# A dense SwiGLU layer whose first tile starts on parts of its input, and whose gate and up products take high and low rows in one moving operand

## The reference

```python
def swiglu(u, wg, wu, wd):
    return (jax.nn.silu(u @ wg) * (u @ wu)) @ wd
...
        x = x + gate * rmsnorm(y, g_norm[l, 1])
        shift, scale, gate = ada_modulation(c, w_ada[l, 1], b_ada[l, 1])
        h = rmsnorm(x, g_norm[l, 2]) * (1.0 + scale) + shift
        if l % 2 == 0:
            y = swiglu(h, w_gate_d[l // 2], w_up_d[l // 2], w_down_d[l // 2])
```

## Time and profile before

| what | value |
|---|---|
| median of three runs | 1752.06 us (1749.61 to 1752.65) |
| the profiled execution, its own time | 1752.9 us |
| its span, first to last instruction | 1751.1 us |
| TensorE busy | 1520.8 us, 87% of the span |
| VectorE, ScalarE, GpSimd busy | 712.4, 545.6, 63.1 us |
| mean granted clock of TensorE | 0.939 of 2.4 GHz |
| dense layer, first to last matmul start | 242.6 to 489.3 us |

### The profile page before, as it was taken

The page is one execution under the profiler, slowest core; times in us unless marked ns, Lnnn a source line. Parts: engine busy times, 40 slices in busy tenths (PEclk is TensorE's granted clock), DMA queues, the critical chain, the costliest instruction groups (busy, mean ns, idle before and its releaser), DMA issues.

```text
span 1751.1 us, 30564 instructions
## 1 busy us (share of the span) xinstructions
PE 1520.8 (87%) x12460; PEld 1226.9 (70%) x12461; DVE 712.4 (41%) x1020; ACT 545.6 (31%) x751; POOL 63.1 (4%) x66
## 2 busy tenths in 40 slices
PE   5999979999989998665658999979997569999794
PEld 3868769999976776554447875579995458888453
DVE  2263164555434532300017871166662036665112
ACT  2134043333222321100007750056551034554101
POOL 0010000000010001000000000000000000000002
PEclk9999989999999999887879999999998879999897
DMA  9625456545443436499999998997668995555694
GB/s 358 258 104 241 182 228 265 193 169 193 155 153 107 168 145 271 185 424 423 424 425 426 412 384 360 426 389 282 246 260 324 424 420 224 217 223 234 272 425 147
DMA packets 74565, 488.97 MB, mean 279 GB/s; under 512 B 9792, under 2 KB 13920, under 8 KB 16544
## 3 DMA queue, kind: packets, MB, share of 16 engines
q1 hardware_dynamic: 72176, 479.94, 68.1%
q10 hardware_dynamic: 1648, 4.59, 0.8%
q0 software_dynamic: 576, 2.10, 0.4%
HBM read 482.66 MB, written 3.93 MB: 278 GB/s over the span
## 4 chain that ended last, share of the span: by engine, by line
PE 78%; DMA 10%; issue 5%; DVE 3%; ACT 2%; POOL 1%; SPq 1%; ACTq 0%; POOLq 0%; DVEq 0%
PE PG L1315 9%; DMA ring<-in_experts 6%; PE Y L914 5%; PE PG L1359 5%; PE PG L1425 5%; PE TRB L1359 4%; PE Y L1327 4%; PE Y L1387 4%; PE Y L922 3%; PE Y L1176 3%; PE PG L878 3%; PE PG L879 3%; PE PG L880 3%; PE TRB L1365 3%; PE PG L1365 3%
## 5 line engine op out<-in xcount | busy, mean ns | idle before, releaser
L1315 PE MATMUL PG<-ring,mixT 128*32 128x128 f32 (+1 forms) x1920 | 120.7, 351 | 73.5 <-issue 73.5
L1315 PEld LDWEIGHTS PG<-ring,mixT 128*32 128x32 f32 (+1 forms) x1920 | 91.2, 138 | 105.7 <-issue 90.8
L1508 ACT ACTIVATE parts<-ring 128x2048 fp32r<-128x2048 f32 x84 | 158.4, 1906 | 11.8 <-PE Y L880 8.2
L2306 DVE COPY arena<-TRB 128x64 f32<-128x64 f32 (+1 forms) x70 | 17.6, 251 | 338.6 <-PE TRB L1301 338.6
L1508 ACT ACTIVATE rope<-PG 64x128 f32<-64x128 f32 (+2 forms) x84 | 27.1, 323 | 374.2 <-PE PG L1315 350.8
L1315 PE MATMUL PG<-arena,mixT 128*32 128x128 f32 (+1 forms) x1664 | 103.3, 358 | 38.7 <-issue 38.7
L878 PE MATMUL PG<-h_parts,parts 128*128 128x256 f32 x448 | 127.5, 285 | 10.2 <-DVE parts L2182 10.2
L879 PE MATMUL PG<-h_parts,parts 128*128 128x256 f32 x448 | 127.4, 284 | 0.0
L880 PE MATMUL PG<-h_parts,parts 128*128 128x256 f32 x448 | 127.2, 284 | 0.0
L1315 PEld LDWEIGHTS PG<-arena,mixT 128*32 128x32 f32 (+1 forms) x1664 | 80.4, 142 | 65.8 <-issue 51.9
L2182 DVE TENSOR_TENSOR parts<-ring,parts 128x2048 fp32r<-128x2048 f32 x42 | 95.9, 2292 | 25.5 <-ACT parts L1508 25.4
(11 more groups left out here) (361 smaller groups left out, 2750.3 us busy)
## 6 DMA issues: line engine op xcount, KB each, us to landing
ring<-in_experts SPq DMA_DIRECT2D x168, 1024.0 KB, 12.2
arena<-in_experts SPq DMA_DIRECT2D x168, 1024.0 KB, 15.8
ring<-in_weights SPq DMA_DIRECT2D x116, 1024.0 KB, 6.1
ring<-in_weights SPq DMA_DIRECT2D x4, 512.0 KB, 4.3
ypairs<-hT ACTq DMA_DIRECT2D x3, 512.0 KB, 6.3
tok<-in_x SPq DMA_DIRECT2D x1, 1024.0 KB, 9.1
result<-scr SPq DMA_DIRECT2D x2, 512.0 KB, 2.6
ring<-in_weights SPq DMA_DIRECT2D x2, 432.0 KB, 5.9
```

The lines of the kernel that those rows point to most:

```text
L1315: last = mm(bank[i * n:(i + 1) * n, 0:width], xe[:, k, 0:n], w[k // 4][:, k % 4, i * width:(i + 1) * width], start=(k == 0), stop=(k == KD ...
L1508: return nc.scalar.activation(out_, in_, func, **kw)
```

## The change

Four things are done.

- The post norms of both mixers and of the dense layer are fed sooner: ScalarE squares each block of Y when it is done (the last down tile signals `y_pair` three times), and for the mixers TensorE sums the first two blocks (four matmuls) ahead of the last projection block.
- ScalarE's and VectorE's splits of weight units 0 and 1 move ahead of the dense layer's pre norm; on ScalarE they stand between the squares of the post norm. ScalarE writes the high part of h straight from hT plus shift, in eight pieces, VectorE the low part in eight; the separate copies fall away.
- Tile 0 (`gu_first`) takes the high pieces of h for gate as each is ready, then up, then the low pieces. Its count of matmuls is unchanged.
- In tiles 1 to 27 the two products with the high weights (h high, h low) become one matmul of 512 columns, whose halves go to the two halves of a bank; gate has one bank, up the other. ScalarE then copies both low halves out (128 x 512), VectorE adds the high halves (128 x 512), and silu and the multiplication follow. TensorE waits for that sum (`gu_summed`) before the next gate and up tile; its wait for `act_ready` there falls away.

```diff
@@ -226,6 +226,7 @@
 
 OUT_ORDER = (2, 3, 0, 1)
 MIX_EARLY, MIX_LATE = (0, 1, 5, 6, 7), (2, 3, 4)
+POST_ORDER = [2 * c + j for c in OUT_ORDER for j in range(2)]
 
...
@@ -428,8 +429,8 @@
         qks = scr[:, 0:6, :]
         kro = scr[:, 6, :]
 
-        act = cut("dense", 2, T)
-        sg = cut("dense", 2, T)
+        gu_sum = cut("dense", 4, T).rearrange("p (a m) t -> p a m t", a=2)
+        low_part = cut("dense", 2, T)
         act_parts = parts[:, 0:4 * T].rearrange("p (a b t) -> p a b t", a=2, b=2)
         act_hi, act_lo = act_parts[:, 0, :, :], act_parts[:, 1, :, :]
         w_parts = [parts[:, 4 * T + i * KD * SW:4 * T + (i + 1) * KD * SW] for i in range(2 * SPLITS)]
...
@@ -814,18 +817,26 @@
                 for _ in range(n):
                     mm(bank[:, 0:T], ident, con[:, C_IOTA:C_IOTA + T], start=True, stop=True)
 
-            def stats(kind, n, q, between=None):
-
-
-                bank = take_tr((kind, n, "partial"))
-                if (kind, n) == ("pre", 3):
-                    busy(bank, 6)
-                for k in range(KD):
-                    if k % 2 == 0:
-                        pe.wait_ge(sq_ready, 4 * q + k // 2 + 1)
+            def partial(kind, n, q, at, to):
+
+                if at == 0:
+                    bank = take_tr((kind, n, "partial"))
+                    if (kind, n) == ("pre", 3):
+                        busy(bank, 6)
+                bank = tr[TR.bank((kind, n, "partial"))]
+                for i in range(at, to):
+                    k = POST_ORDER[i] if kind == "post" and n != 1 else i
+                    if i % 2 == 0:
+                        pe.wait_ge(sq_ready, 4 * q + i // 2 + 1)
                     g = 32 * (k % 4)
-                    last = mm(bank[g:g + 32, 0:T], ones[:, 0:32], scr[:, k, :], start=(k < 4), stop=(k >= 4))
-                last.then_inc(tr_full, 1)
+                    last = mm(bank[g:g + 32, 0:T], ones[:, 0:32], scr[:, k, :], start=(i < 4), stop=(i >= 4))
+                if to == KD:
+                    last.then_inc(tr_full, 1)
+
+            def stats(kind, n, q, between=None, at=0):
+
+
+                partial(kind, n, q, at, KD)
                 if between:
                     ada_rows(between)
                 bank = take_tr((kind, n, "total"))
...
+            def gu_first():
+
+                for d in range(2):
+                    pe.wait_ge(split_lo, d + 1)
+                    for k in range(KD):
+                        if d == 0:
+                            pe.wait_ge(h_ready, KD + k + 1)
+                        c = slice(k * SW, k * SW + P)
+                        mm(PG[:, d, 0:T], w_hi[d][:, c], h_hi[:, k, :], start=(k == 0), stop=False, skip_group_check=True)
+                        mm(PG[:, d, 0:T], w_lo[d][:, c], h_hi[:, k, :], start=False, stop=False, skip_group_check=True)
+                for k in range(KD):
+                    pe.wait_ge(h_lo_ready, k + 1)
+                    for d in range(2):
+                        last = mm(PG[:, d, T:2 * T], w_hi[d][:, k * SW:k * SW + P], h_lo[:, k, :],
+                                  start=False, stop=(k == KD - 1), skip_group_check=True)
+                return last
+
...
             def gu_tile(t):
 
-                bank = PG[:, t % 2, :]
+                if t == 0:
+                    return gu_first()
+                pe.wait_ge(gu_summed, t)
                 for m in range(2):
                     d = dense_use(KINDS[m], t // 2)
                     pe.wait_ge(split_lo, d + 1)
                     for k in range(KD):
-                        if t == 0 and m == 0 and k % (KD // 2) == 0:
-                            pe.wait_ge(h_lo_ready, k // (KD // 2) + 1)
-                        last = split_product(bank[:, m * T:(m + 1) * T], d % SPLITS, (h_hi[:, k, :], h_lo[:, k, :]),
-                                             k * SW + t % 2 * P, k == 0, k == KD - 1)
+                        c = slice(k * SW + t % 2 * P, k * SW + t % 2 * P + P)
+                        mm(PG[:, m, :].rearrange("p (i t) -> p i t", i=2), w_hi[d % SPLITS][:, c], h_parts[:, :, k, :],
+                           start=(k == 0), stop=False, skip_group_check=True)
+                        last = mm(PG[:, m, 0:T], w_lo[d % SPLITS][:, c], h_hi[:, k, :],
+                                  start=False, stop=(k == KD - 1), skip_group_check=True)
                 return last
 
...
@@ -900,6 +931,8 @@
                 for k in range(KD):
                     last = split_product(Yk[:, k, :], d % SPLITS, (act_hi[:, t % 2, :], act_lo[:, t % 2, :]),
                                          t % 2 * D + k * P, t == 0 and k % 2 == 0, t == FT - 1)
+                    if t == FT - 1 and k % 2 and k < KD - 1:
+                        last.then_inc(y_pair, 1)
                 return last
...
@@ -1197,6 +1230,8 @@
                 for b in range(2):
                     sc_over(2 + b)
                     pe.wait_ge(pj_free[b], len(PJ_LAYER) // 2 * (l + 1))
+                    if b:
+                        partial("post", 2 * l, 4 * l + 1, 0, KD // 2)
                     mixed(b, MIX_EARLY)
                     mixed(b, MIX_LATE).then_inc(y_full if b else out_read, 1)
...
@@ -1220,12 +1255,10 @@
 
 
             mixer(0)
-            stats("post", 0, 1)
+            stats("post", 0, 1, at=KD // 2)
             stats_pre(1, 2)
...
@@ -1525,9 +1558,14 @@
                     ae.wait_ge(hx_ready, KD * n + k + 1)
                     run(hT[:, k, :], hT[:, k, :], ACT.Identity, bias=mod[:, n, k:k + 1]).then_inc(h_ready, 1)
 
-            def squares_post(n, ready, value):
-                ae.wait_ge(ready, value)
-                for j in range(4):
+            def squares_post(n, *js):
+                for j in js:
+                    if n == 1:
+                        ae.wait_ge(*((y_pair, j + 1) if j < 3 else (down_done, FT)))
+                    elif j == OUT_ORDER[-1]:
+                        ae.wait_ge(y_full, 2 + n // 2)
+                    else:
+                        ae.wait_ge(out_read, (D // SW - 1) * (n // 2) + OUT_ORDER.index(j) + 1)
                     run(scr[:, 2 * j:2 * j + 2, :], Yk[:, 2 * j:2 * j + 2, :], ACT.Square).then_inc(sq_ready, 1)
 
...
             def split(d):
 
                 u = slot_of_dense(d)
@@ -1689,28 +1724,35 @@
                 run(w_hi[d % SPLITS], ring[:, slot_of[u], :, :].rearrange("p k c -> p (k c)"),
                     ACT.Copy).then_inc(split_hi, 1)
 
-            for i in range(2):
-                k = slice(i * KD // 2, (i + 1) * KD // 2)
-                ae.wait_ge(h_ready, KD + (i + 1) * KD // 2)
-                run(h_hi[:, k, :], hT[:, k, :], ACT.Copy).then_inc(h_hi_ready, 1)
-            for d in range(3):
-                split(d)
+            ae.wait_ge(*tr_done("mt4", 0))
+            squares_post(0, *OUT_ORDER[0:2])
+            split(0)
+            squares_post(0, OUT_ORDER[2])
+            split(1)
+            squares_post(0, OUT_ORDER[3])
+            squares_pre(1)
+            ada_rows(ADA_NORM[1])
+            for k in range(KD):
+                ae.wait_ge(hx_ready, KD + k + 1)
+                run(h_hi[:, k, :], hT[:, k, :], ACT.Identity, bias=mod[:, 1, k:k + 1]).then_inc(h_ready, 1)
+            split(2)
             for t in range(FT):
                 ae.wait_ge(gu_full, t + 1)
-                if t >= 2:
-                    ae.wait_ge(act_ready, t - 1)
-                run(sg[:, t % 2, :], PG[:, t % 2, 0:T], ACT.Silu).then_inc(silu_done, 1)
+                ae.wait_ge(gu_summed, t)
+                run(low_part, PG[:, :, T:2 * T], ACT.Copy).then_inc(low_out, 1)
+                ae.wait_ge(gu_summed, t + 1)
+                run(gu_sum[:, t % 2, 0, :], gu_sum[:, t % 2, 0, :], ACT.Silu).then_inc(silu_done, 1)
                 if t == 2:
                     ada_rows(ADA_DENSE)
                 for d in split_after(t):
                     split(d)
-            squares_post(1, down_done, FT)
...
@@ -2174,8 +2216,7 @@
                 mark(V.tensor_scalar(lam_v[:, l, 1:2], lam_v[:, l, 1:2], -LAM0[l], None, ALU.add))
             settle()
             mixer(0)
-            post(0)
-            pre(1)
+
             def split(d):
 
                 ve.wait_ge(split_hi, d + 1)
@@ -2183,21 +2224,27 @@
                                 ring[:, slot_of[slot_of_dense(d)], :, :].rearrange("p k c -> p (k c)"),
                                 w_hi[d % SPLITS].bitcast(F32), ALU.subtract).then_inc(split_lo, 1)
 
-            for i in range(2):
-                k = slice(i * KD // 2, (i + 1) * KD // 2)
-                ve.wait_ge(h_hi_ready, i + 1)
-                V.tensor_tensor(h_lo[:, k, :], hT[:, k, :], h_hi[:, k, :].bitcast(F32), ALU.subtract).then_inc(h_lo_ready, 1)
-            for d in range(3):
+            for d in range(2):
                 split(d)
+            post(0)
+            pre(1)
+            for k in range(KD):
+                ve.wait_ge(h_ready, KD + k + 1)
```

(12 more changed lines are left out.)

15 lines of the change are left out of this document (6 added, 9 removed).

## The result

| | before | changed |
|---|---|---|
| median, four runs each | 1752.11 us (1749.61 to 1752.65) | 1729.62 us (1726.26 to 1730.23) |
| profiled execution, its own time | 1752.9 | 1729.92 |
| its span | 1751.1 | 1728.1 |
| mean granted clock | 0.939 | 0.944 |

A forecast was written before the change was run, and what follows sets the result against it. It took the dense layer as bound by the number and spacing of its matmuls. Gains of 6.3 + 4.8 - 0.5 + 0.9 + 0.5 = 12.0 us gave 1740.9, as median 1740.0; range 1735 to 1747.

The forecast's parts named there:

- The start (6.3): Start of the dense layer: early weight splits let tile 1 start at 244.7 us, 6.3 us sooner, despite a later norm.
- The uncovered evacuation: Between dense tiles 0 and 1: tile 1 starts 1.7 us after tile 0's last matmul's start, with no down tile covering.
- Tiles 1 to 27 (4.8): Dense layer: each pair of 256-column matmuls becomes one of 512 columns at 0.2275 us, 4.8 us less in all.
- Tile 27 and the norms (-0.5, 0.9, 0.5): Tile 27's activations: 0.5 us more; post norm behind the dense layer 0.9 less, behind layer 1's mixer 0.5 less.
- (c): Dense tiles: the evacuation is not covered by the down tile, 27 us in all, 1767 us; chance 0.06.
- (a): Dense tiles 1 to 27: the wide matmul saves nothing, 7.2 us gained in all, 1744.9 us; chance 0.12.
- (b): Dense start: low clock for all of tile 0, and again after the 1.7 us pause; 8.0 gained, 1744.1 us; chance 0.10.
- (d): Layer 1 or the experts: the gain is given back waiting for weights at a fixed time, 1752 us; chance 0.06.
- Theory 2: From the experiments, not the prediction: experts start 11 us sooner and meet clock and DMA in another phase.

The follow-up runs named there:

- experiment 7: Changed kernel with ScalarE's copy of the low rows done twice per dense tile, then four times: 1740.50 us and 1743.23 us.
- place 68: Start of TensorE's experts loop in its listing, counted modulo 256: kernel before, 1752.11 us; changed kernel with 95 added waits, 1739.89 us.
- place 229: Same count, modulo 256: changed kernel, 1729.62 us, again 1730.32; kernel before with 161 instructions jumped over, 1741.92 us, or as executed waits, 1742.27.

## Why the prediction was right and wrong

**The start (6.3): right, 6.2.** The first matmul came at 234.2 us and tile 1 at 243.2; without the 1.6 us that the unchanged code ahead gained that is 235.8 and 244.8, against 235.3 and 244.7. The norm was 1.4 late, not 1.6 (218.68 plus the 1.6, against 218.86). Two errors cancel: the clock was also low from 220.8 to 224.2, inside the norm, which the sum put at nothing (the modulation product took 4.49 us instead of 3.66), and in tile 0 it was low for 3.4 us, not 4.5. The uncovered evacuation was right: tile 1 starts 1.69 us after tile 0's last matmul's start, 1.7 counted. Splits that fill a wait pay although they make the norm later, because h had to wait for the norm, and the first product for the splits.

**Tiles 1 to 27 (4.8): mis-sized, 2.5.** The step took 0.2275 us from 512-column products that follow each other. Here each alternates with a 256-column one, and the pair takes 0.3505 (5.608 / 16); less the 0.1188 of the narrow one (5.701 / 48) the wide one costs 0.2317. The prediction's own second reading, 0.231 from the line through 256 and 384 columns, was the right one, and it chose the other; the rest is the narrow product, taken at 0.1193 as the mean over both kinds of tile. The formula on the page "TensorE: Matmul & The Clock Gate" of the Trainium skill (section "Back-to-back issue gap"), which the page gives for a single matmul, would make it 2.5 ns a pair (the prediction has 2.6); measured are 2 x 118.8 - 231.7 = 5.9 ns, nearer to it than the 11.1 taken, and still more than double.

**Tile 27 and the norms (-0.5, 0.9, 0.5): about right.** 0.2 was lost at tile 27; with the norm behind the dense layer the stretch gained 3.4 less 2.5, that is 0.9 where 0.4 stood; layer 1's mixer 0.7, where 0.5 stood. That last one is luck in part: the early squares gained more than was counted, and the partial sums, counted as a gain, cost 0.8. The prediction set their price right, at 0.9, and overlooked that they buy nothing: once the squares are early, two sums are left behind the last square also when none is moved, as it had counted itself for the dense layer's norm.

**Rivals.** (c) didn't come: 1.35 us were spare. (a) holds by half. (b) didn't: after the pause of 1.41 us at tile 1 the clock stayed at 1.00, here and in all variants with that pause; in the two with pauses of 1.9 and 2.9 us (experiment 7) it fell. (d) was the only place in which the prediction looked at the later stages, and it asked only whether the gain could be lost to DMAs.

**The step that failed** is the one that isn't there: the sum sets the experts and the end at nothing, as work that "moves along". Some 10 of the 22.5 us come from there. Cause: 863 instructions fewer ahead of the loop over the experts move its code from place 68 to 229. Shown from both sides: the kernel before at place 229 takes 9 us less, the changed one at place 68 takes 10 more. At equal places the change is worth 1741.9 - 1730.3 = 11.6 us (place 229, one sitting) and some 10 to 12 at place 68 (1749.4 or 1752.1, less 1739.9): the 12.0 of the sum, partly by errors that cancel (1.6 of luck ahead, 2.3 too much for the wide products).

The Trainium skill's page "Runtime: NRT & Kernel Launch" (section "Instruction fetch mechanics") has instructions fetched in blocks of 16 KiB, 256 instructions, one after the other, and a taken branch whose target lies outside the blocks held stalls until that block has come. The trace agrees with the size (16,384 bytes, one to 254 executed in straight code), and the two runs with 256 instructions jumped over agree with a period of 256. A stall costs 4.4 us here ahead of expert 3, 6.4 ahead of expert 7, and 4.6 where the loop is left.

**Open** stays which branch misses which block at each place (the count has no real block edge in it), and what else moves a run: kernels of place 229 differ by up to 10 us from the last norm on (1042.6 to 1052.3, half of it ScalarE's stall above; 1042.6 to 1049.3 without that run), and unchanged code ahead of layer 0's projection ends 1.6 us apart. Theory 2, the phase, may be worth some of these 7 us; no run isolates it, and it doesn't explain the 9 and 10 us above. The edit moved the code of other engines too: at a branch in expert 6 VectorE pauses for 5.3 to 5.6 us in the three kernels made from the one before and in none made from the changed one. It was covered there, since expert 6 takes 210.0 to 210.6 us in the first and 209.4 to 210.7 in the others.

## What to carry to other kernels

If an engine branches at run time, an edit ahead of the branch moves the code behind it, and that alone can be worth as much as the edit. Compare such kernels at equal places (instructions that are jumped over do it without being executed), read "issue" waits at each branch in both traces, and then look for a better place. Here only TensorE's code was moved on purpose. And split a time by stages before it is taken for an answer: two runs here came out at the expected total for another reason, one missed it though its term was right, and one hid that a part of the change costs time.

## What the runs showed of the hardware

- TensorE's instructions come in packets of 16,384 bytes, and where they stand relative to the code sets some 10 us of 1750, which their share (some 120 packets, 0.4% of the DMA engines' time) doesn't suggest.
- A stall at a branch costs twice on TensorE: 4.42 us, and then 2.44 us since 64 products run in part at the lower clock level of 1.2 GHz (9.57 against 7.13 us).
- ScalarE pauses at branches too: 5.4 us from a branch to the next instruction in one kernel, where 0.2 pass in the changed one; and 4.9 to 6.1 us at a branch in expert 6 in every kernel.
- An instruction that only waits, for something already there, takes TensorE 0.108 us (first product of the changed kernel at 18.69 us with 160 of them, at 11.69 with 95).
- A 512-column product (fp32r, two runs of 256) costs 0.2317 us between 256-column ones, and 0.2275 among its like.
